# Rows of u and of the FFN activations pitched 1088 columns, and real tokens half a 256-byte line from the weights

## What is computed

```
h = concat(meta, x)                                           # (1040, 1024)
h = h + 0.5 * swiglu(rms_norm(h), w_gu (1024 x 5632), w_down (2816 x 1024))
u = rms_norm(h)
h = h + (g_fox * fox_attention(u) @ w_bf + g_mla * latent_attention(u) @ w_bm) @ w_out
h = h + 0.5 * swiglu(rms_norm(h), w_gu2, w_down2)
return h[16:]
```

## Time and profile before

| | |
|---|---|
| three timed executions | 2940.70, 2946.58 and 2927.48 us, median 2940.7 |
| profiled execution | span 2942.3 us; no other time of that execution is given, and the span stands for it |
| TensorE busy | 2806.3 us of the span (95%), 13970 matmuls |
| VectorE, ScalarE, GpSimd busy | 1078.9, 664.0 and 747.4 us |
| TensorE clock granted over the span | 0.918 of full speed |

### The profile page before, as it was taken

The page is one execution under the profiler, slowest core; times in us unless marked ns, Lnnn a source line. Parts: engine busy times, 40 slices in busy tenths (PEclk is TensorE's granted clock), DMA queues, the critical chain, the costliest instruction groups (busy, mean ns, idle before and its releaser), DMA issues. The chain is left out here.

```text
span 2942.3 us, 37535 instructions
## 1 busy us (share of the span) xinstructions
PE 2806.3 (95%) x13970; PEld 2404.2 (82%) x13970; DVE 1078.9 (37%) x1994; ACT 664.0 (23%) x1237; POOL 747.4 (25%) x711
## 2 busy tenths in 40 slices
PE   7999999999979999998899998999879999999999
PEld 7999999999977878876577776888668888888887
DVE  5332222222554424242466663111142333333334
ACT  4111111110243223222344443112131111111110
POOL 3212211121132222221244445221232222222220
PEclk8999999999986858667799999999989999999999
DMA  3111111111110000000000001110312111111111
GB/s 125 58 44 48 54 44 44 44 44 37 55 61 1 23 22 0 1 1 28 8 6 3 5 1 65 43 50 14 116 44 64 43 58 43 43 57 43 43 36 58
DMA packets 32463, 115.67 MB, mean 39 GB/s; under 512 B 4000, under 2 KB 5920, under 8 KB 32208
## 3 DMA queue, kind: packets, MB, share of 16 engines
q1 hardware_dynamic: 32336, 113.90, 11.6%
HBM read 105.09 MB, written 8.65 MB: 39 GB/s over the span
## 5 line engine op out<-in xcount | busy, mean ns | idle before, releaser
L52 PE MATMUL f_bank<-u_hi,f_w_hi 128*128 128x346 f32 (+2 forms) x1760 | 618.5, 351 | 15.9 <-POOL u_lo L211 13.2
L53 PE MATMUL f_bank<-u_hi,f_w_lo 128*128 128x346 f32 (+2 forms) x1760 | 619.4, 352 | 0.0
L54 PE MATMUL f_bank<-u_lo,f_w_hi 128*128 128x346 f32 (+2 forms) x1760 | 618.8, 352 | 0.0
L424 POOL TENSOR_TENSOR f_w_lo<-f_raw,f_w_hi 128x1024 fp32r<-128x1024 f32 x132 | 326.9, 2496 | 1126.2 <-ACT f_w_hi L366 1126.0
L52 PEld LDWEIGHTS f_bank<-u_hi,f_w_hi 128*128 128x128 f32 x1760 | 332.5, 189 | 48.9 <-issue 17.0
L53 PEld LDWEIGHTS f_bank<-u_hi,f_w_lo 128*128 128x128 f32 x1760 | 332.3, 189 | 30.8
L54 PEld LDWEIGHTS f_bank<-u_lo,f_w_hi 128*128 128x128 f32 x1760 | 332.8, 189 | 30.0
L502 DVE TENSOR_TENSOR f_work<-f_work,f_bank 128x346 f32<-128x346 f32 (+2 forms) x110 | 64.4, 585 | 798.2 <-PE f_bank L54 788.1
L52 PE MATMUL f_bank<-f_hid_hi,f_w_hi 128*128 128x346 f32 (+2 forms) x880 | 309.0, 351 | 0.0
L53 PE MATMUL f_bank<-f_hid_hi,f_w_lo 128*128 128x346 f32 (+2 forms) x880 | 308.9, 351 | 0.0
L54 PE MATMUL f_bank<-f_hid_lo,f_w_hi 128*128 128x346 f32 (+2 forms) x880 | 308.9, 351 | 0.0
(11 more groups left out here) (279 smaller groups left out, 4571.6 us busy)
## 6 DMA issues: line engine op xcount, KB each, us to landing
f_raw<-in_ffn SPq DMA_DIRECT2D x132, 512.0 KB, 3.4
gt_raw<-in_gate SPq DMA_DIRECT2D x24, 512.0 KB, 3.5
fox_raw<-in_fox SPq DMA_DIRECT2D x12, 512.0 KB, 4.4
kept_hsave<-h_in SPq DMA_DIRECT2D x1, 4160.0 KB, 13.0
h_out<-kept_hsave SPq DMA_DIRECT2D x8, 520.0 KB, 6.6
ld_xin<-in_x SPq DMA_DIRECT2D x8, 512.0 KB, 4.4
op_raw<-in_wout SPq DMA_DIRECT2D x8, 512.0 KB, 5.7
out<-f_raw SPq DMA_DIRECT2D x6, 512.0 KB, 3.7
```

What stands on the lines that cost most here:

```text
L52: nc.tensor.matmul(out, w_hi, x_hi, start=first, stop=False)
L53: nc.tensor.matmul(out, w_lo, x_hi, start=False, stop=False)
L54: return nc.tensor.matmul(out, w_hi, x_lo, start=False, stop=last)
L424: nc.gpsimd.tensor_tensor(w_lo[:, slot, :], raw[:, raw_slot, :], w_hi[:, slot, :].bitcast(F32), ALU.subtract).then_inc(wlo_done, 1)
```

## The change

The rows of `u_hi`, `u_lo`, `hid_hi` and `hid_lo` become 1088 columns long, 4352 bytes or 17 lines exactly, and the tokens in them begin at column 16. Every tensor is followed by a filler up to a multiple of 256 bytes, and a lead-in tensor sets the first one at 224 within its line, so that all tensors begin at 224. Weights then begin at 224, token 0 of every row at 32 (place 64) and token 16, the first real one, at 96 (place 128). The three chunks become 272, 384 and 384 columns: token 0 is at place 64, tokens 272 and 656 are at place 128. The chunks of 512 are at place 128. The fox stage takes the same chunks in this order, where it had 384, 384, 272; the latent attention keeps its own. The buffers for DMA descriptors are made smaller to make room.

```diff
-ALL_TOKENS = [(0, 348), (348, 346), (694, 346)]
+ALL_TOKENS = [(0, 272), (272, 384), (656, 384)]
+ROW = 1088
+LEAD = 16
+LINE = 256
+def columns(t0, n):
+    return slice(LEAD + t0, LEAD + t0 + n)
+def placed(nc, stack, prefix):
+    def tensor(name, shape, dt=F32):
+        made = stack.enter_context(nc.sbuf_tensor(prefix + name, shape, dt))
+        over = 4 * math.prod(shape[1:]) % LINE
+        if over:
+            stack.enter_context(nc.sbuf_tensor(prefix + name + "_fill", [P, (LINE - over) // 4], F32))
+        return made
+    return tensor
...
-        hid_hi = sb("hid_hi", [P, 2, 2, T], F32R)
-        hid_lo = sb("hid_lo", [P, 2, 2, T], F32R)
+        hid_hi = sb("hid_hi", [P, 2, 2, ROW], F32R)
+        hid_lo = sb("hid_lo", [P, 2, 2, ROW], F32R)
...
                                 last = mm3(nc, out[:, 0:n], w_hi[:, slot, k * P:(k + 1) * P],
-                                           w_lo[:, slot, k * P:(k + 1) * P], g.u_hi[:, k, t0:t0 + n],
-                                           g.u_lo[:, k, t0:t0 + n], k == 0, k == KD - 1)
+                                           w_lo[:, slot, k * P:(k + 1) * P], g.u_hi[:, k, columns(t0, n)],
+                                           g.u_lo[:, k, columns(t0, n)], k == 0, k == KD - 1)
...
+FOX_TILES = [(0, 128, 144), (0, 128, 256), (0, 128, 256)]
...
                 def scale(u):
                     is_q, c = units[u]
-                    t0, n = QK_TOKENS[c]
+                    t0, n = ALL_TOKENS[c]
...
-                    wait(pe, vt_done, p, 3, b + 1)
+                    wait(pe, vt_done, p, 3, min(b + 2, 3))
...
-        g.u_hi = sb("u_hi", [P, KD, T], F32R)
-        g.u_lo = sb("u_lo", [P, KD, T], F32R)
+        g.u_hi = sb("u_hi", [P, KD, ROW], F32R)
+        g.u_lo = sb("u_lo", [P, KD, ROW], F32R)
...
+        start = -(-nc.sbuf_base // 32) * 32
+        s.enter_context(nc.sbuf_tensor("lead", [P, (224 - start) % LINE // 4], F32))
+        sb = placed(nc, s, "")
...
-    nc = bacc.Bacc("TRN2", target_bir_lowering=False, num_devices=1)
+    nc = bacc.Bacc("TRN2", target_bir_lowering=False, num_devices=1, dynamic_dma_scratch_size=1024)
```

More of the change, by code:

```diff
@@ L10 @@
+import math
 from contextlib import ExitStack
@@ L204, in act_hi @@
             act.wait_ge(self.u_done, i + 1)
-            self.nc.scalar.copy(self.g.u_hi[:, i % KD, t0:t0 + n], self.u32[i % 4][:, 0:n]).then_inc(self.hi_done, 1)
+            self.nc.scalar.copy(self.g.u_hi[:, i % KD, columns(t0, n)], self.u32[i % 4][:, 0:n]).then_inc(self.hi_done, 1)
     def lo(self, eng, i):
@@ L210, in lo @@
         eng.wait_ge(self.hi_done, i + 1)
-        return eng.tensor_tensor(self.g.u_lo[:, k, t0:t0 + n], self.u32[i % 4][:, 0:n],
-                                 self.g.u_hi[:, k, t0:t0 + n].bitcast(F32), ALU.subtract)
+        return eng.tensor_tensor(self.g.u_lo[:, k, columns(t0, n)], self.u32[i % 4][:, 0:n],
+                                 self.g.u_hi[:, k, columns(t0, n)].bitcast(F32), ALU.subtract)
     def pool_lo(self, pool, c):
@@ L465, in down @@
                         last = mm3(nc, bank[4 + v % 4][:, 0:n], w_hi[:, slot + f, d * P:(d + 1) * P],
[L466 to L467 removed]
+                                   w_lo[:, slot + f, d * P:(d + 1) * P], hid_hi[:, parity, f, columns(t0, n)],
+                                   hid_lo[:, parity, f, columns(t0, n)], f == 0, f == 1)
                     last.then_inc(down_ready, 1)
@@ L674, in _ @@
                     last = mm3(nc, acc[c][:, 0:n], w_hi[:, k * P:(k + 1) * P], w_lo[:, k * P:(k + 1) * P],
-                               g.u_hi[:, k, t0:t0 + n], g.u_lo[:, k, t0:t0 + n], k == 0, k == KD - 1)
+                               g.u_hi[:, k, columns(t0, n)], g.u_lo[:, k, columns(t0, n)], k == 0, k == KD - 1)
                 last.then_inc(ready, 1)
@@ L755, in _ @@
                         last = mm3(nc, bank[j][:, 0:n], w_hi[:, j, k * P:(k + 1) * P],
-                                   w_lo[:, j, k * P:(k + 1) * P], g.u_hi[:, k, t0:t0 + n],
-                                   g.u_lo[:, k, t0:t0 + n], k == 0, k == KD - 1)
+                                   w_lo[:, j, k * P:(k + 1) * P], g.u_hi[:, k, columns(t0, n)],
+                                   g.u_lo[:, k, columns(t0, n)], k == 0, k == KD - 1)
                     last.then_inc(ready, 1)
@@ L1097, in sums @@
                         wait(pe, exp_done, p, PW, 0)
-                    for i, off in enumerate(QK_TILES[c]):
+                    for i, off in enumerate(FOX_TILES[c]):
                         last = nc.tensor.matmul(SUM[:, NH * i:NH * i + NH], p32[:, u % 2, off:off + P],
@@ L1944, in mixed_hi @@
                     act.wait_ge(shut, 4 * t + 2 * (c + 1))
-                    nc.scalar.copy(g.u_hi[:, t, META + 512 * c:META + 512 * c + 512],
+                    nc.scalar.copy(g.u_hi[:, t, columns(META + 512 * c, 512)],
                                    o_tile(t)[:, 512 * c:512 * c + 512]).then_inc(uhi_done, 1)
@@ L1984, in tile @@
                             last = mm3(nc, out[:, :], w_hi[:, j, k * P:(k + 1) * P], w_lo[:, j, k * P:(k + 1) * P],
-                                       g.u_hi[:, k, t0:t0 + 512], g.u_lo[:, k, t0:t0 + 512], k == 0, k == KD - 1)
+                                       g.u_hi[:, k, columns(t0, 512)], g.u_lo[:, k, columns(t0, 512)], k == 0, k == KD - 1)
                     else:
@@ L2003, in mixed_lo @@
                     dve.wait_ge(uhi_done, KD * c + t + 1)
-                    x = slice(META + 512 * c, META + 512 * c + 512)
+                    x = columns(META + 512 * c, 512)
                     nc.vector.tensor_tensor(g.u_lo[:, t, x], o_tile(t)[:, 512 * c:512 * c + 512],
@@ L2095, in _ @@
                         last = mm3(nc, bank[u % 4][:, :], w_hi[:, m % 3, k * P:(k + 1) * P],
-                                   w_lo[:, m % 3, k * P:(k + 1) * P], g.u_hi[:, k, t0:t0 + n],
-                                   g.u_lo[:, k, t0:t0 + n], k == 0, k == KD - 1)
+                                   w_lo[:, m % 3, k * P:(k + 1) * P], g.u_hi[:, k, columns(t0, n)],
+                                   g.u_lo[:, k, columns(t0, n)], k == 0, k == KD - 1)
                     last.then_inc(ready, 1)
@@ L2149, in build @@
             g.rot = mb("rot", [P, P])
-            with nc.sbuf_tensor("h_in", [P, KD, T], F32) as h, nc.sbuf_tensor("sumsq_in", [P, T], F32) as sumsq:
-                g.h, g.sumsq = h, sumsq
+            with ExitStack() as stream:
+                hb = placed(nc, stream, "")
+                g.h, g.sumsq = hb("h_in", [P, KD, T]), hb("sumsq_in", [P, T])
                 load_phase(nc, g)
@@ L2169, in build @@
             gate_phase(nc, g)
-        with nc.sbuf_tensor("h_out", [P, KD, T], F32) as h, nc.sbuf_tensor("sumsq_out", [P, T], F32) as sumsq:
-            g.h, g.sumsq = h, sumsq
+        with ExitStack() as stream:
+            hb = placed(nc, stream, "")
+            g.h, g.sumsq = hb("h_out", [P, KD, T]), hb("sumsq_out", [P, T])
             out_proj_phase(nc, g)
```

53 lines of the change are left out of this document (25 added, 28 removed).

## The result

The changed kernel takes 2967.0 us in the median of 14 runs (2950.1 to 2975.6), the kernel before beside it 2933.9 (14 runs, 2927.5 to 2948.3). The ratio is 1.009, with a 95% interval of 1.0072 to 1.0108. (The two medians alone would give 1.011: most executions of before lie near 2932 or near 2947, and its median falls into the lower group.) The prediction was 2914, a gain of 0.9%, in a range of 2830 to 2975: the range holds the time, the direction is wrong.

The account below looks back on a forecast made before the run. TensorE's matmul rate was taken to bound the two FFNs. From the 2942.3 us span, 36.2 less for places and 9.2 more for fox waits gave 2915.3, 2913.7 against the median; predicted 2914, range 2830 to 2975.

Parts of the forecast that it names:

- Constant place at 512 columns: Second FFN, gate (u) and output projection: matmuls settle at 227.5 ns at place 128; 13.9 and 4.8 us less.
- First FFN: Set of three chunks falls from 475.8 to 467.3 ns over 1584 sets: 13.5 us less.
- Fox products: Fox stage: 576 matmuls 4.3 ns cheaper and 288 matmuls 2.4 ns cheaper, 3.2 us less.
- `lt` and `fg`: These two small stages: 96 sets of chunks, 8.5 ns cheaper each, 0.8 us less.
- First maximum: Fox, V0 at k = 7: TensorE's 0.93 us wait for VectorE's `split_lo` grows by 1.5 us in each of four pairs.
- `values(1)`: Fox: transposes wait for ACT's copy of the last v chunk, 0.8 us more in each of four pairs.
- B: Rival, chance 0.20: rate depends on place alone, settling gives nothing; 232.7 ns at 512 columns, first FFN -6.7 us, 2946 us.
- C: Rival, chance 0.16: constant place settles on the dear value, decided by over 233.5 ns at 512 columns; 2985 us, 1.5% more.
- A: Rival, chance 0.22: constant half line keeps moving and weight reads apart, removing much of the matmul surplus; 2800 to 2885 us.
- D: Rival, chance 0.08: place does not matter, the four-row pattern has another source, only the waits remain; 2951 us.
- the rule named beside it: Trainium skill: weight load and moving operand have independent read ports, so place could not matter; gives D's 2951 us.

Follow-up runs that it names:

- e3: Changed kernel with chunks 384, 384, 272, old fox order, every tensor at 224, 48 columns ahead (real tokens at place 0): ratio 0.993 to before.
- e5: Changed kernel with chunks 384, 384, 272, old fox order, every tensor at 224, no columns ahead (real tokens at place 64): ratio 0.993 to before.
- e4: Changed kernel with chunks 384, 384, 272, old fox order, every tensor at 224, 16 columns ahead (real tokens at 128): 232.2 ns per second-FFN matmul.
- e6: Changed kernel with only v of the fox stage back in the old chunk order and its old wait: 2957.1 us, ratio 1.0051 to before.
- stream program: Separate program, 48 matmuls of one kind back to back, other engines idle, per place and width: at 512 columns 226.7 ns at place 0, 232.5 at 128.
- e2: Kernel before with only the new chunks and new fox order, neither pitch nor fillers: 2963.6 us, ratio 1.0081 to before.

## Why the prediction was wrong

- **The bound was right.** TensorE's rate sets the FFNs, before and after. Changing the place changes their length and leaves no idle time (620.00 of 620.00 us in e3, e5 and e4).
- **Constant place at 512 columns: the step that failed.** The prediction took 227.5, "because at 384 columns the places 0 and 128 are equally cheap". The 227.5 was a settled value of place 0 at 512 columns, and the rows at 384 columns were single visits of three matmuls in a stream that kept moving. Neither carries over: a stream that stays at 128 has 232.5 at 512 columns (176.0 at 384, against 173.5 at place 0). Of the 18.7 us forecast for second FFN, gate and output projection, none came: 0.0, +0.4 and +1.1. The row that lay at the right place and width, 232.7 for k = 2, stood in the text as the other near row, and it was the nearer one. That may be luck: it is a single visit too, and the single visit to 128 at 384 columns, 173.3, misses the settled 176.0.
- **First FFN: forecast -13.5, measured +2.2.** A set of three chunks was to cost 467.3 and costs 175.6 x 2 + 126.7 = 477.9, the 478.3 that the prediction gave for the chunks alone. The settled value for 384 columns at 128 (175.6 for 171.5) is 8.2 of the 10.6 ns, and the 272 columns at place 64 (126.7 for 124.3) 2.4.
- **Fox products, -3.2, and `lt` and `fg`, -0.8.** In fox the two long chunks were at place 0, because of the allocation, and cost 173.0 to 173.5 ns, 123.5 for the short one: 576 x 2.5 + 288 x 3.2 = 2.4 us less than the prediction's rates of before. That gain is inside the stage's +15.6. `lt` and `fg` took 2.5 more together.
- **First maximum: mechanism right.** 2.4 us of idle time were forecast and 2.23 measured; the growth was 1.3 us a pair for 1.5. The 0.6 us of waits inside V1 were not forecast.
- **`values(1)`: right.** 0.8 forecast, 0.6 measured.
- **The clock behind the wait: missing.** The prediction priced the wait and not what follows it: 1.6 us in each V1 at the lower clock, 6.4 us in all. With the waits of 4 x (1.3 + 0.6 + 0.6) = 10.0 us that is 16.4 us, of which some is given back; the stage lost 15.6. e6 shows that the lower clock goes with the short V0. That the sum comes out near 15.6 is not a proof of each term: the last pair loses more than its terms and the others less.
- **The rivals.** B, at chance 0.20, had the second FFN right (232.7 against 232.2), but its gain of 6.7 us in the first FFN did not come. C's deciding rate of 233.5 at 512 columns was not reached in the second FFN of after; the gate's 233.3 and the 233.2 of e6's second FFN came near. A was refuted: no place of the stream program is below 226.7. D, and the rule named beside it, fell with the same program and with e3's 17.4 us.

In sum: forecast -36.2 for places and +9.2 for waits; measured about zero for places and +15.6 in the fox stage, and the rest of the 25.3 us in other stages. Of these, mla's +4.3 is no more than two executions of equal code differ by. `fg` has 46.6 to 46.8 us in all four kernels with the new chunks and 44.9 to 46.3 in the six others, so its +1.8 belongs in part to the chunks. That the time fell inside the range of 2830 to 2975 is due to the range's width, which took in part of C, and not to the forecast.

## What to carry to other kernels

A stream of matmuls of 512 columns ran up to 6% slower or faster by the distance between its weights and its moving rows, so before a layout is changed, the settled rate is to be measured at the very distance and width that are wanted, some 50 matmuls of each. A sample from a stream whose distance moves, or from another width, does not stand for it. And when an edit makes TensorE arrive sooner at an operand that another engine still has to make, the price can be more than that wait: here a pair lost 1.3 us to it, 1.2 to later waits and 1.6 at a lower clock behind it, and whether the clock falls has to be looked up for each such wait.

## What was not expected of the hardware

- **The distance counts in steps of 4 bytes, and its effect depends on the width.** At 512 columns the rate runs from 226.7 ns (places 0, 28, 240, 252) to 240.0 (place 20), and at places 0 and 128 it is the same, within 1.3 ns, for weights that begin at 0, 32, 128 and 224.
- **A rate settles in one of several cycles.** The same place and width gave 232.2 or 233.2 at 512 columns (second FFN of after and e6), and 173.3 or 176.7 at 384 columns and place 192. What chooses the cycle is open; e3's first FFN, in the dearer one, takes 5 us more than e5's.
- **A floor below 256 columns.** 128, 160, 192 and 224 columns all take 111.5 ns a matmul with its own weight load (5.35 / 48), 272 take 123 to 127 (place 192 and 64). A chunk made narrower than 224 columns saves nothing in such a stream.
- **2.2 us of idle time, and the next 4.6 us at a mean clock of 0.63**, in a stream that had been busy before; 1.1 us had no such effect. But 1.94 us of idle time were followed by 0.63 in the first pair of e2 and by 1.00 in its fourth.
- **The mla stage took from 370.5 to 392.3 us in code of the same instructions.** For the same stretch of work (1848 matmuls) the granted clock goes with it: after 0.89, e6 0.92.

```profile
1427.60:1808.70 381.10, 355.30 (x1848) 271.05 (x1848) 231.74 (x521) 154.49 (x398) 152.69 (x308) 0.89 0.01 4
```
```profile
1415.50:1786.10 370.60, 344.74 (x1848) 263.73 (x1848) 233.10 (x521) 154.26 (x398) 152.72 (x308) 0.92 0.01 4
```

The two kernels have the same code and the same addresses in that stage. Which is cause and which effect is open, and no run was made for it. There is one profiled execution of each, so a spread of some 10 us may lie in any one span, which is the reason why no difference of a few us is claimed here from spans alone.
